# One condition in the emitter of a transformer-block kernel: which neighbours on TensorE are separated by a wait for TensorE's own last write

## The reference, cut to what matters

```python
h = rms_norm(x, norm1_g[l]) * (1 + scale1) + shift1
z = h @ w_in[l]
q, k, v, p, g_attn, g_pool = jnp.split(z, split_at, axis=-1)
q = rms_norm(heads(q), q_norm_g[l]); k = rms_norm(heads(k), k_norm_g[l])
attn = moba_attention(q, k, heads(v), rel_bias)     # own block of 256 keys + the 3 best past blocks
pool = multiscale_pool(p.reshape(B, S, POOL_GROUPS, POOL_GROUP_W))
pool = jnp.einsum('bsgc,gcd->bsgd', pool, pool_w[l]).reshape(B, S, POOL_W) * pool_scale[l]
merged = (jax.nn.sigmoid(g_attn) * (attn @ w_branch_attn[l])
          + jax.nn.sigmoid(g_pool) * (pool @ w_branch_pool[l]))
x = x + gate1 * (merged @ w_out[l])
h2 = rms_norm(x, norm2_g[l]) * (1 + scale2) + shift2
u = causal_dwconv(h2 @ w_up[l], conv_w[l], conv_b[l])
u_g, u_v = jnp.split(u, 2, axis=-1)
x = x + gate2 * ((jax.nn.silu(u_g) * u_v) @ w_down[l])
```

## Time and profile before

| | us |
|---|---|
| median of 3 runs | 1965.44 |
| the profiled execution, its own time | 1962.53 |
| its span (core 0, the slowest) | 1961.0 |
| TensorE busy in that span | 1742.9 (89%) |
| weight loads (PEld), beside the matmuls | 1187.6 (61%) |
| VectorE / ScalarE / GpSimd busy | 1092.0 / 1075.4 / 657.1 |

### The profile page before, as it was taken

The page is one execution under the profiler, slowest core; times in us unless marked ns, Lnnn a source line. Parts: engine busy times, 40 slices in busy tenths (PEclk is TensorE's granted clock), DMA queues, the critical chain, the costliest instruction groups (busy, mean ns, idle before and its releaser), DMA issues.

```text
span 1961.0 us, 39762 instructions; the slowest of 8 cores (1943.7 to 1961.0 us)
## 1 busy us (share of the span) xinstructions
PE 1742.9 (89%) x13621; PEld 1187.6 (61%) x13700; DVE 1092.0 (56%) x1486; ACT 1075.4 (55%) x1395; POOL 657.1 (34%) x609
## 2 busy tenths in 40 slices
PE   7768999989987989796989999989976999999998
PEld 3335555555554767665666777754435888887443
DVE  1556555555555564645364554426765888887222
ACT  1436454544535978776777988953234666665000
POOL 1778667667671000000000000005764444442000
PEclk9889999999997999998989999989997999999999
DMA  9894444434455141424232130414759534340332
GB/s 257 161 184 138 115 120 130 116 110 123 119 115 123 46 89 29 114 58 109 64 79 51 18 58 2 86 44 138 198 129 167 51 36 41 37 41 11 107 115 95
DMA packets 245742, 187.49 MB, mean 96 GB/s; under 512 B 158293, under 2 KB 211925, under 8 KB 244457
## 3 DMA queue, kind: packets, MB, share of 16 engines
q1 hardware_dynamic: 186378, 154.93, 28.6%
q0 software_dynamic: 59168, 30.02, 12.8%
HBM read 170.77 MB, written 44.12 MB: 110 GB/s over the span
## 4 chain that ended last, share of the span: by engine, by line
PE 75%; issue 5%; DMA 5%; ACT 4%; POOL 4%; DVE 4%; SPq 1%; DVEq 0%; ACTq 0%; POOLq 0%
PE psum L387 72%; ACT arena L395 3%; PE psum L391 3%; POOL arena L403 2%; DMA arena<-ada_w 2%; POOL arena L441 2%; SPq L400 1%; DVE arena L403 1%; DMA arena<-w_in 1%; DVE psum L403 1%; ACT arena L419 1%; DMA arena<-SGS 1%; DMA arena<-xw 1%; DVE arena L414 1%; POOL arena L439 1%
## 5 line engine op out<-in xcount | busy, mean ns | idle before, releaser
L387 PE MATMUL psum<-arena 128*128 128x256 bf16 (+7 forms) x12493 | 1661.4, 291 | 158.9 <-ACT arena L395 73.2
L387 PEld LDWEIGHTS psum<-arena 128*128 128x128 bf16 (+3 forms) x12572 | 1119.9, 99 | 685.4 <-issue 265.8
L395 ACT ACTIVATE arena<-psum 128x1024 bf16<-128x1024 f32 (+2 forms) x731 | 636.9, 962 | 355.5 <-PE psum L387 282.9
L403 POOL TENSOR_TENSOR arena<-arena 128x1024 bf16<-128x1024 f32 (+2 forms) x211 | 347.4, 1653 | 315.8 <-ACT arena L395 144.9
L414 DVE SCALAR_TENSOR_TENSOR arena<-psum,arena 128x512 f32<-128x512 f32 (+1 forms) x354 | 266.1, 753 | 85.2 <-PE psum L387 65.1
L403 DVE TENSOR_TENSOR arena<-psum,arena 128x512 f32<-128x512 f32 (+5 forms) x245 | 151.2, 636 | 278.6 <-PE psum L387 146.0
L414 DVE SCALAR_TENSOR_TENSOR arena<-arena 128x1024 f32<-128x1024 f32 (+3 forms) x137 | 209.2, 1532 | 73.6 <-DMA arena<-ada_w 32.7
L395 ACT ACTIVATE arena<-psum,arena 128x512 f32<-128x512 f32 (+4 forms) x220 | 162.2, 737 | 140.8 <-PE psum L387 138.8
L400 POOL DMA_DIRECT2D arena<-wba x1 | 0.8, 768 | 615.6 <-PE psum L387 615.6
L395 ACT ACTIVATE arena<-arena 128x512 bf16<-128x512 f32 (+3 forms) x174 | 144.3, 829 | 88.7 <-DVE arena L403 52.3
L441 POOL TENSOR_TENSOR arena<-arena 128x8 f32<-128x8 f32 (+1 forms) x148 | 185.5, 1257 | 15.8 <-POOL arena L439 0.6
(11 more groups left out here) (24 smaller groups left out, 146.2 us busy)
## 6 DMA issues: line engine op xcount, KB each, us to landing
arena<-xw SPq DMA_DIRECT2D x80, 512.0 KB, 4.3
arena<-ada_w SPq DMA_DIRECT2D x32, 512.0 KB, 4.8
arena<-wup POOLq DMA_DIRECT2D x44, 256.0 KB, 5.3
arena<-ada_w SPq DMA_DIRECT2D x8, 1024.0 KB, 11.4
arena<-w_in POOLq DMA_DIRECT2D x8, 1024.0 KB, 17.7
VS<-arena SPq DMA_DIRECT2D x32, 256.0 KB, 4.2
KS<-arena SPq DMA_DIRECT2D x32, 256.0 KB, 4.2
SGS<-arena SPq DMA_DIRECT2D x8, 1024.0 KB, 6.1
```

Of the source, the lines that this page charges most:

```text
L387: P.op('tensor', lambda e: e.matmul(out, lhsT=lhsT, rhs=rhs, start=start, stop=stop), R, W, dur=d, mode=(rk(lhsT.shape[0]), rk(fs(lhsT)), ...
L395: P.op('scalar', lambda e: e.activation(out=out, in_=in_, func=func, **kw), R, W, dur=edur('scalar', fs(in_)) + (0.1 if 'accum_out' in kw ...
L403: P.op(eng, lambda e: e.tensor_tensor(out=out, in0=in0, in1=in1, op=op), R, W, dur=edur(eng, fs(out)))
```

## The change

The loop in emit() gets one more condition. A changed mode no longer leads to a wait if both neighbours use 128 rows and neither is float32. Modes still differ for 64-row and 32-row operands and for float32, and there the wait stays. The scheduler's own cost for a mode change is as before.

```diff
--- before.py
+++ after.py
@@ -217,7 +217,7 @@
         prev = None
         for o in self.ops:
             if o.eng == 'tensor' and not o.is_dma:
-                if prev is not None and prev.mode != o.mode:
+                if prev is not None and prev.mode != o.mode and not (prev.mode[0] == o.mode[0] == 128 and not prev.mode[2] and not o.mode[2]):
                     o.force = prev
                     prev.flag = True
                 prev = o
```

## The result

The changed kernel took 1953.8 us (median of 11 runs), the kernel before 1965.0 beside it (11 runs). The ratio is 0.9942, with an interval of 0.9922 to 0.9962: 0.58% faster, 11 us (8 to 15), where I had forecast 24. The profiled execution took 1955.5 us, with a span of 1953.9. Averaged over the eight cores of the two profiled executions, the span fell from 1953.0 to 1942.5 us.

The account below looks back on a forecast made before the run. TensorE was taken to bound most of the kernel up to 1470 us. Discounted gains of 1.1 (loads), 11.1 (projections), 7.0 (attention), 3.1 (branch stage) and 1.6 (fulfilled waits) made 24 us, giving 1941 us; range 1930 to 1956.

Parts of the forecast that it names:

- The price of a bound wait: At TensorE's switches between matmuls and transposes: each own wait that binds costs 0.31 us, all of it won.
- an already fulfilled own wait: At 30 switches where another engine ends last, TensorE's own wait still costs 0.10 us, 3.0 us at most.
- the feed-forward part: Last 490 us, 94.9% matmuls in the chain, no switch the change could touch: length unchanged.
- Rival 1: At bare switches the array drains by itself, 0.15 us won each: 12.5 us gained, 1953 us; chance 0.15.
- rival 4: At the freed switches another wait ends at the same instant, so time stays at 1965 us; chance 0.05.
- Rival 3: Fewer, longer TensorE waits in projections and attention drop the clock, 68 us more at 1.2 GHz: 1971 us; chance 0.04.
- the signs that the prediction named: Profile checks, including less TensorE idle from 140 to 1345 us; wrong if projections shorten by less than 6 us.
- Rival 2: Engines behind TensorE take back the projections' and loads' gain, L387 waiting longer: about 10 us, 1955 us; chance 0.08.
- Attention: Attention stage: 28 binding waits on the chain at 0.312 us, 80% kept, gain 7.0 us.
- let the same share of the gain be lost: Each stage's gain cut by other engines' chain share: 48% loads, 24% projections, 20% attention, 29% branch stage.
- the 96 places: Binding own waits on the chain: 7 loads, 47 projections, 28 attention, 14 branch stage; 30.0 us before discount.
- those waits begin from matmuls that come earlier now: Argument that waits for VectorE (17.6 us, projections) and ScalarE (69.3 us, attention) move forward with TensorE.

Follow-up runs that it names:

- e1: Kernel before with TensorE's own waits removed in attention alone (32 places); ratio 0.9981 to the kernel before.
- e5: Changed kernel with the shift1 and shift2 additions left out; ratio 0.9745 to the kernel before.
- e4: Kernel before, own waits kept, with the shift1 and shift2 additions left out; ratio 0.9851 to the kernel before.
- e6: Changed kernel with the shift1 addition in the projections moved from GpSimd to VectorE; ratio 0.9796 to the kernel before.
- e3: Changed kernel whose scheduler no longer adds 0.4 for switches that need no wait; ratio 0.9813 to the kernel before.

## Why the prediction was off by half

**What held.** The price of a bound wait (0.31 us), that it goes entirely, that an already fulfilled own wait costs 0.10 us beside another, that the feed-forward part stays as it is: the rows above show each. Rival 1 (the array drains itself, a remainder of 0.16 us per switch) and rival 4 (nothing happens) fall with the steps of 0.05 and 0.22 us. The Trainium skill, TensorEngine Tiling (Array Packing), Key Properties, says that a change of the tiling mode drains TensorE; no bare switch here leaves room for a drain, so the transpose flag does not act as such a mode. Rival 3 falls: 148 us at 1.2 GHz before and 151 after, where it needed 68 more.

**Its own signs.** Two of the signs that the prediction named speak against it: the projections shortened by 5.3 us, under the 6 below which it called itself wrong, and TensorE's idle time on core 7 from 140 to 1345 us (133.3 before) fell by 1.3 us. Rival 2's sign came for VectorE (17.6 to 23.9 us) and not for ScalarE's exponential (69.3 and 69.4).

**Attention** was forecast at 7.0 us and gave 4.4 (6.7 without the clock, which was at 1.2 GHz for 6 us more there; e1 8.0, e5 against e4 6.3). ScalarE's idle time after the mask transposes, 1.02 us in the earlier trace rows, shows how the gain comes through:

```profile
1100.99 7.01 PE L387 MATMUL psum<-arena 128*128 128x256 bf16 x60 [0.29 <-ACT arena L395]
1107.84 1.06 PE L391 MATMUL psum<-arena 128*96 128x128 bf16 x16
...
1109.49 1.94 ACT L395 ACTIVATE arena<-psum 128x1024 bf16<-128x1024 f32 x2 [0.39 <-PE psum L387]
```

It is 0.39 us now. 0.63 of it went, two waits of 0.31: ScalarE, on whose exponentials attention hangs, got its scores that much earlier.

**The step that failed** is "let the same share of the gain be lost": the discount of the 96 places by the share of other engines in the chain. For the projections it kept 76%, 11.1 us; they gave 5.3 (4.4 without the clock). For the loads it kept 1.1, and from 50 to 140 us nothing came; for the branch stage 3.1, and it gave 1.4 (0.7). In these three the mechanism of rival 2 is what happened, which I gave 0.08: what TensorE saves largely comes back at its next wait for VectorE, GpSimd or ScalarE's copies. That rival's number, 1955 us, is 1 from the measured 1953.8, but by luck in its parts: it had nothing from the projections and 3.1 us from the branch stage. The measured time also lies inside the range given, 1930 to 1956, only because the range's upper end took in rivals 1 and 2; the forecast's own sum does not reach it. I had argued against rival 2 that "those waits begin from matmuls that come earlier now". That holds for the sum of the head norm alone. It does not for the product that stands before it in VectorE's queue, which is tied to GpSimd's additions and through them to transposes a whole tile earlier.

**Why the chain did not tell.** Its piece before, at that place:

```profile
188.69 4.71 PE psum L387 x21
193.40 0.02 issue
193.42 0.69 DVE arena L615
```

The chain steps from VectorE's sum (L615) back into TensorE, since a matmul that ended at 193.40 was the last update of a semaphore that it could find before the sum, and gives TensorE 4.71 us. The full record says otherwise. By the order of the waits, the squares that this sum reads were ready at 191.33 (ScalarE's L395); VectorE's two wait instructions nearest to the sum were over by 193.11 and 193.21, before that matmul ended, and VectorE was busy with the product until 193.50, as the rows above show (190.26 + 3.24; the shown ends overlap by 0.08 us). It had no idle time before the sum at all. It was held by the product, and the product by GpSimd's addition. How much this hides can be read from the record of before: followed back in the same way, but stepping to an engine's own preceding instruction wherever VectorE, ScalarE or GpSimd had no idle time, core 7's chain from 140 to 624 us gives L387 and L391 47.7% instead of 65.8%, the product (L414) 8.7% instead of 0.4%, and GpSimd's L403 8.2% instead of 2.7%. In attention TensorE's share falls only from 75.8 to 72.5%. The same view could have told it: at each step into TensorE, look at what the waiting engine did in the microsecond before.

What stays open: how much of the projections' loss comes from this loop and how much from the head norm's own chain (power and last product). e4, e6 and e3 change both by moving the whole order; that about 80% and not 100% came through in e6, and 60% in e5, leaves room for it, and for ScalarE's copies, for which TensorE waits more after the change. In the branch stage I have no pair that isolates it: there the own waits pay 1.3 us without the additions (e4 to e5) and 1.4 with them, and the 4.1 us that come back before GpSimd's L403 show where, but not why.

## What to carry to other kernels

A gain on the engine that is 90% busy is worth what the loops through the other engines leave of it; before adding such gains up, follow one period of the stage from the bound engine back to itself and compare the periods of all loops, and for each step of the chain into the bound engine ask whether the waiting engine was free at that moment. If two paths are nearly equal, change the second one too: here the same edit gave 5 us of the projections alone and 13 behind a one-word move of the additions. Before reading a difference of stages from one execution, look at the clock of every core in it. And once a cost is gone from the kernel, take it out of the scheduler's model as well: with e3's one condition the gain went from 0.6 to 1.9%.

## What the runs showed of the hardware

- A bf16 transpose and a bf16 matmul of the same 128x128 shape follow each other as equals do: 55 to 56 ns after a transpose, 109 after 256 columns, 216 after 512.
- A VectorE product of 128x1024 with two inputs in SBUF takes 1.28 us, and up to 3.46 beside a GpSimd addition of the same size (core 7 before): started while the addition runs, it ends 1.08 to 1.09 us after it. The mean over the projections was 1972 ns before and 1276 with no additions on GpSimd. I had not looked at such stretching at all.
- The same addition takes 2.35 us on GpSimd and 1.22 on VectorE, so moving it to the busier engine shortened the kernel by 1.5% (e6 against the change alone).
